# Two transformer blocks in one program: other order at the start, at each stage's end, in the RWKV scan and at the last store

## The reference, cut to what matters

```
for i in 0, 1:                                  # first block; mixer = gMLP, then RWKV-7
    h = h + 0.5 * rms_norm(swiglu(rms_norm(h, g[0]), w13, w2), g[1])      # ffn
    h = h + rms_norm(mixer(rms_norm(h, g[2])), g[3])
    h = h + 0.5 * rms_norm(swiglu(rms_norm(h, g[4]), w13', w2'), g[5])    # ffn
    gate = sigmoid(rms_norm(h, g[6]) @ w_gate)
    h = h + rms_norm(gate * (p[i] @ w_proj), g[7])                        # ple
# second block: the same form, mixer = dilated attention, then windowed GQA
rms_norm(x, g) = x * rsqrt(mean(x*x) + eps) * g
# RWKV-7: per head a 64 x 64 state, S_t = S_{t-1} diag(w) + (S_{t-1} a) b^T + v k^T, y_t = S_t r_t,
# then y minus its mean per head, times rsqrt of its variance, + bonus, times g, @ w_out
```

## Time and profile before

| | before |
|---|---|
| median of 3 runs, us | 2353.99 (2350.56 to 2355.45) |
| profiled execution: own time, us | 2350.35 |
| profiled execution: span, us | 2348.6 |
| mean granted TensorE clock | 0.984 |
| busy share of the span, PE / DVE / ACT / POOL | 96% / 63% / 49% / 8% |
| mean DMA rate, GB/s | 168 |

### The profile page before, as it was taken

The page is one execution under the profiler, slowest core; times in us unless marked ns, Lnnn a source line. Parts: engine busy times, 40 slices in busy tenths (PEclk is TensorE's granted clock), DMA queues, the critical chain, the costliest instruction groups (busy, mean ns, idle before and its releaser), DMA issues.

```text
span 2348.6 us, 33586 instructions
## 1 busy us (share of the span) xinstructions
PE 2251.9 (96%) x13285; PEld 1824.1 (78%) x13285; DVE 1471.0 (63%) x2077; ACT 1156.9 (49%) x1670; POOL 181.9 (8%) x289
## 2 busy tenths in 40 slices
PE   8999899999999899889999999999999999979998
PEld 6888788887888557768887888877887788748886
DVE  5656657656664866566657656656656765647655
ACT  5445445445544454244455445455445544545444
POOL 1001001001000110410011001001001000051001
PEclk9999999999999999899999999999999999989999
DMA  7556555554755540046456555524555655506553
GB/s 246 188 189 210 181 181 192 181 180 152 225 189 200 174 136 3 3 160 204 163 193 200 189 187 190 183 91 158 189 186 170 206 180 194 176 13 202 190 175 107
DMA packets 289755, 395.60 MB, mean 168 GB/s; under 512 B 11673, under 2 KB 193249, under 8 KB 289601
## 3 DMA queue, kind: packets, MB, share of 16 engines
q1 hardware_dynamic: 284752, 377.20, 48.4%
q0 software_dynamic: 4704, 16.20, 2.0%
q10 hardware_dynamic: 144, 0.07, 0.0%
HBM read 392.37 MB, written 1.05 MB: 168 GB/s over the span
## 4 chain that ended last, share of the span: by engine, by line
PE 78%; DVE 6%; ACT 2%; issue 2%; POOL 1%; DMA 0%; DVEq 0%; POOLq 0%; SPq 0%; ACTq 0%
PE bank L504 23%; PE bank L506 23%; PE bank L505 22%; PE bank L530 1%; DVE wl L800 1%; PE bank L518 1%; ACT wh L616 1%; DVE TMP L842 0%; ACT XH L628 0%; DVE H L862 0%; DVE qPS L1830 0%; PE bank L1404 0%; ACT JUNK L623 0%; PE bank L2471 0%; PE bank L2482 0%
## 5 line engine op out<-in xcount | busy, mean ns | idle before, releaser
L800 DVE TENSOR_TENSOR wl<-raw,wh 128x1024 fp32r<-128x1024 f32 x708 | 860.4, 1225 | 570.7 <-ACT wh L616 570.2
L616 ACT ACTIVATE wh<-raw 128x1024 fp32r<-128x1024 f32 x708 | 744.4, 1058 | 658.5 <-PE bank L506 630.1
L504 PE MATMUL bank<-wh,XH 128*128 128x512 f32 x2000 | 805.4, 403 | 18.5 <-ACT wh L616 6.0
L505 PE MATMUL bank<-wl,XH 128*128 128x512 f32 x2000 | 784.3, 392 | 0.0
L506 PE MATMUL bank<-wh,XL 128*128 128x512 f32 x2000 | 784.1, 392 | 0.0
L504 PEld LDWEIGHTS bank<-wh,XH 128*128 128x128 f32 x2000 | 378.5, 189 | 109.9 <-issue 19.4
L506 PEld LDWEIGHTS bank<-wh,XL 128*128 128x128 f32 x2000 | 378.4, 189 | 82.5
L505 PEld LDWEIGHTS bank<-wl,XH 128*128 128x128 f32 x2000 | 379.3, 190 | 73.3 <-issue 0.5
L504 PE MATMUL bank<-wh,AH 128*128 128x512 f32 x704 | 276.0, 392 | 0.0
L506 PE MATMUL bank<-wh,AL 128*128 128x512 f32 x704 | 274.1, 389 | 0.0
L505 PE MATMUL bank<-wl,AH 128*128 128x512 f32 x704 | 274.0, 389 | 0.0
(11 more groups left out here) (332 smaller groups left out, 1709.7 us busy)
## 6 DMA issues: line engine op xcount, KB each, us to landing
raw<-in_ffn_w_dram SPq DMA_DIRECT2D x184, 512.0 KB, 4.7
raw<-in_ffn_wi_dram SPq DMA_DIRECT2D x176, 512.0 KB, 4.7
raw<-in_ffn_w_dram SPq DMA_DIRECT2D x40, 1024.0 KB, 4.9
raw<-in_ffn_wo_dram SPq DMA_DIRECT2D x40, 1024.0 KB, 4.8
raw<-in_a_wqkv_dram SPq DMA_DIRECT2D x18, 1024.0 KB, 4.8
raw<-in_a_w_in_dram SPq DMA_DIRECT2D x16, 1024.0 KB, 6.1
raw<-in_b_w_in_dram SPq DMA_DIRECT2D x12, 1024.0 KB, 4.9
bc<-in_norm_g_dram POOLq DMA_DIRECT2D x16, 512.0 KB, 5.2
```

The lines of the kernel that those rows point to most:

```text
L504: pe.e.matmul(o, a, h, start=(k == 0), stop=False)
L505: pe.e.matmul(o, a, l, start=False, stop=False)
L616: act.e.activation(self.wh[j % N_W][:, 0:p.size], self.raw[p.chunk % N_RAW][:, p.at:p.at + p.size], ACT.Copy).then_inc(*self.rounded.up(j))
L800: dve.e.tensor_tensor(self.wl[j % N_W][:, 0:p.size], self.raw[p.chunk % N_RAW][:, p.at:p.at + p.size], self.wh[j % N_W][:, 0:p.size].bitca ...
```

## The change

- Start: SP loads tile 0, chunk 0 in four DMAs of 256 KB (part 0's two first, with a semaphore of their own), then tile 1, then the rest. TensorE turns only tile 0 ahead of the first step and tile 1 at steps 2 and 3. ACT and DVE put parts 0 and 1 ahead of tile 1.
- Stage ends: the sum of squares is a function of its own, `dve_mean`, ahead of `dve_weigh` of the second half. In PLE stages `dve_weigh` doesn't wait for the square. In the dilated stage the same for both tiles.
- Scan: both grams ahead of both `krv`; the banks are handed out from the pair after V's last one; the norm's segments are steps of their own and spread over levels 3 to 5 and `fin`; tile 1's bonus is made ahead of `seen 1`, into KK's tile 0; the leave of part 6 moves from `fin` into the tail; the tail's two halves are interleaved and TensorE's turns stand beside steps 15 and 19.
- End: four stores of 256 KB, each when its half has been added.

The diff, cut to its core:

```diff
     def pe_turn_own(self, pe, n, step):
 
-        if n and step == 6:
+        first = 6 if n else 2
+        if step == first:
             self.pe_turn_x(pe, n, 1, 0)
-        if n and step == 7:
+        if step == first + 1:
             self.pe_turn_x(pe, n, 1, 1)
...
+    def wait_raw(self, e, p):
+        if p.j:
+            e.wait_ge(self.d_raw[p.chunk % N_RAW], p.chunk)
+        else:
+            e.wait_ge(self.d_first, 1)
...
         for j in range(N_W):
+            if j < 2:
+                self.act_x_hi(act, 0, 0, j)
+            if j == 2:
+                for b in range(2):
+                    self.act_x_hi(act, 0, 1, b)
             self.round(act, j)
...
-        dve.wait_ge(self.squared, "out", n, b, t)
+        if STAGES[n][0] != "ple":
+            dve.wait_ge(self.squared, "out", n, b, t)
         dve.e.tensor_tensor(self.TMP[:, t, b, 512:1024], y, self.bct[g][:, b * 512:(b + 1) * 512],
                             ALU.mult).then_inc(*self.weighed.up(n, b, t))
...
-    def dve_resid(self, dve, n, t):
+    def dve_mean(self, dve, n, t):
...
+    def dve_resid(self, dve, n, t):
+
+        x = self.cols(T, "sm", n)[:, t:t + 1]
...
         for t in range(T):
+            self.dve_mean(dve, n, t)
             self.dve_weigh(dve, n, 1, t, self.pair((n, "out", 1))[t])
             self.dve_resid(dve, n, t)
...
         dve.e.memset(self.NEG[:, :], -0.5).then_inc(*self.neg.up())
         for b in range(2):
-            for t in range(T):
-                self.dve_x_scale(dve, 0, t, b)
-                self.dve_x_lo(dve, 0, t, b)
-        for j in range(N_W):
+            self.dve_x_scale(dve, 0, 0, b)
+        self.dve_x_lo(dve, 0, 0, 0)
+        self.leave(dve, 0)
+        self.dve_x_lo(dve, 0, 0, 1)
+        self.leave(dve, 1)
+        self.dve_x(dve, 0, 1)
+        for j in range(2, N_W):
             self.leave(dve, j)
...
+        if c == 0:
+            to = to.rearrange("p k (s n) -> p k s n", s=2)
+            for i, (k0, s) in enumerate(((0, 0), (0, 1), (2, 0), (2, 1))):
+                signal = self.d_first.up(s, by=16) if k0 == 0 else self.d_raw[0].up(*(("half", 0), (0,))[s], by=16)
+                sp.e.dma_start(to[:, k0:k0 + 2, s, :], src[:, k0:k0 + 2, s, :]).then_inc(*signal)
+            return
...
+        tokens(0)
...
+            if c == 0:
+                tokens(1)
...
-            sp.wait_ge(self.resid, n, t, 1)
-            sp.e.dma_start(self.out[0, t * P:(t + 1) * P, :], self.H[:, t, :]).then_inc(*self.d_out.up(t, by=16))
-        sp.wait_ge(self.d_out, T - 1)
+            for b in range(2):
+                sp.wait_ge(self.resid, n, t, b)
+                sp.e.dma_start(self.out[0, t * P:(t + 1) * P, b * 512:(b + 1) * 512],
+                               self.H[:, t, b * 512:(b + 1) * 512]).then_inc(*self.d_out.up(t, b, by=16))
+        sp.wait_ge(self.d_out, T - 1, 1)
...
-        for o in range(2):
-            steps += [("gram", 0, o), ("krv", 0, o)]
-        steps += [("complete", 0)]
+        steps += [("gram", 0, 0), ("gram", 0, 1), ("krv", 0, 0), ("krv", 0, 1), ("complete", 0)]
...
+        steps[-1:-1] = [("bonus", 1, 0), ("bonus", 1, 1)]
+        side = {1: [("state", 1), ("bonus", 0, 0), ("bonus", 0, 1)], 2: [("yo", 0)], 3: [("centre", 0, 0)],
+                4: [("square", 0, 0), ("centre", 0, 1)], 5: [("var", 0, 0), ("square", 0, 1), ("gain", 0, 0)]}
         for lv in range(1, 6):
             steps += [("level_a", 1, 0, lv), ("level_a", 1, 1, lv), ("level_b", 1, 0, lv), ("level_b", 1, 1, lv)]
             steps += side[lv]
-        steps += [("fin", 1, 0), ("fin", 1, 1), ("seen", 2), ("turn", 0, 0), ("turn", 0, 1), ("state", 2)]
+        steps += [("fin", 1, 0), ("var", 0, 1), ("gain", 0, 1), ("fin", 1, 1), ("scale", 0, 0), ("add", 0, 0),
+                  ("scale", 0, 1), ("add", 0, 1), ("seen", 2), ("turn", 0, 0), ("turn", 0, 1), ("state", 2)]
...
-    SCAN_TAIL = (("seen", 3), ("bonus", 1, 0), ("bonus", 1, 1), ("yo", 1), ("norm", 1, 0, 0, 6), ("norm", 1, 1, 0, 6),
-                 ("turn", 1, 0), ("turn", 1, 1))
+    SCAN_TAIL = (("seen", 3), ("part", 6), ("yo", 1), ("centre", 1, 0), ("square", 1, 0), ("centre", 1, 1), ("var", 1, 0),
+                 ("square", 1, 1), ("gain", 1, 0), ("var", 1, 1), ("gain", 1, 1), ("scale", 1, 0), ("add", 1, 0),
+                 ("scale", 1, 1), ("add", 1, 1), ("turn", 1, 0), ("turn", 1, 1))
+
+    SCAN_BESIDE = {2: ("seen", 3), 6: ("yo", 1), 15: ("turn", 1, 0), 19: ("turn", 1, 1)}
...
+        self.n_scan = self.place["pair", (n, "v", 1)] + 1
...
-            elif kind == "fin":
-                if tuple(a) == (1, 0):
-                    self.leave(dve, self.layers[n, "out"].parts[6].j)
+            elif kind == "part":
+                self.leave(dve, self.layers[n, "out"].parts[a[0]].j)
...
-        return self.AA if t == 0 else self.TB
-
-    def dve_scan_norm(self, dve, t, h, seg):
+        return self.AA[:, 0, :] if t == 0 else self.KK[:, 0, :]
...
-                    pool.wait_ge(self.product, "yo", 0)
+                    pool.wait_ge(self.product, "bt", 0, 1)
...
-            elif kind == "norm" and a[3] == 6:
-                t, h = a[:2]
+            elif kind == "var":
+                t, h = a
```

More of the change, by code:

```diff
@@ L399, in __init__ @@
         self.d_raw = [count(f"d_raw{i}") for i in range(N_RAW)]
+        self.d_first = count("d_first")
         self.d_bc = [count(f"d_bc{i}") for i in range(3)]
@@ L612, in round @@
         p = self.parts[j]
-        act.wait_ge(self.d_raw[p.chunk % N_RAW], p.chunk)
+        self.wait_raw(act, p)
         if j >= N_W:
@@ L798, in leave @@
         dve.wait_ge(self.rounded, j)
-        dve.wait_ge(self.d_raw[p.chunk % N_RAW], p.chunk)
+        self.wait_raw(dve, p)
         dve.e.tensor_tensor(self.wl[j % N_W][:, 0:p.size], self.raw[p.chunk % N_RAW][:, p.at:p.at + p.size],
@@ L1079, in sync, with tokens @@
             *self.d_g.up(by=16))
-        for t in range(T):
+        def tokens(t):
             sp.e.dma_start(self.H[:, t, :], self.A["x"][0, t * P:(t + 1) * P, :]).then_inc(*self.d_h[t].up(by=16))
+        tokens(0)
         rwkv = self.layers[5, "k"].parts[0].chunk
@@ L1583, in dve_dil_out @@
         parts = self.layers[n, "out"].parts
-        for b in range(2):
-            self.dve_weigh(dve, n, b, 0, self.pair((n, "out", b))[0])
+        self.dve_weigh(dve, n, 0, 0, self.pair((n, "out", 0))[0])
+        self.dve_mean(dve, n, 0)
+        self.dve_weigh(dve, n, 1, 0, self.pair((n, "out", 1))[0])
         self.dve_resid(dve, n, 0)
@@ L2366, in pe_rwkv_scan @@
     def pe_rwkv_scan(self, pe, n):
+        self.n_scan = self.place["pair", (n, "v", 1)] + 1
         for step in self.scan_steps():
             self.pe_scan(pe, *step)
-        beside = {2: 0, 6: 3, 14: 6, 15: 7}
         self.n_pairs = 0
         def during(step):
-            if step in beside:
-                self.pe_scan(pe, *self.SCAN_TAIL[beside[step]])
+            if step in self.SCAN_BESIDE:
+                self.pe_scan(pe, *self.SCAN_BESIDE[step])
             self.pe_turn_next(pe, n, "out", step)
@@ L2622, in act_rwkv_scan @@
                 self.act_decay(act, 1, a[0] - 3, [self.RK[0][:, :], self.RK[1][:, :], self.BT[:, :]])
-            elif kind == "norm" and a[2] == 0:
-                t, h = a[:2]
+            elif kind == "square":
+                t, h = a
                 c = slice(h * 512, (h + 1) * 512)
@@ L2689, in dve_rwkv_scan @@
                 self.dve_scan_complete(dve, *a)
-            elif kind == "norm":
-                t, h, first, end = a
-                for seg in range(first, end):
-                    self.dve_scan_norm(dve, t, h, seg)
+            elif kind in ("centre", "gain", "var", "scale", "add"):
+                self.dve_scan_norm(dve, kind, *a)
             elif kind == "turn":
@@ L2779, in dve_scan_norm @@
                 *self.made.up("centred_y", t, h))
-        elif seg == 2:
+        elif kind == "gain":
             dve.wait_ge(self.figured, "gl", t, h)
@@ L2783, in dve_scan_norm @@
             dve.e.tensor_tensor(x, x, self.GG[:, t, c], ALU.mult).then_inc(*self.made.up("yg", t, h))
-        elif seg == 3:
+        elif kind == "var":
             dve.wait_ge(self.moved, "sq", t, h)
             dve.e.tensor_reduce(var, self.per_head(sq), AX, ALU.add).then_inc(*self.made.up("var", t, h))
-        elif seg == 4:
+        elif kind == "scale":
             dve.wait_ge(self.rs, "gn", t, h)
```

20 lines of the change are left out of this document (8 added, 12 removed).

## The result

| | before | after |
|---|---|---|
| median of the runs | 2353.64 us (2350.56 to 2355.45) | 2322.97 us (2319.10 to 2329.22) |
| ratio | 1 | 0.987 (95%: 0.985 to 0.990) |
| profiled execution: own time, span | 2350.35, 2348.6 | 2319.10, 2317.3 |
| TensorE busy, mean granted clock | 96%, 0.984 | 97%, 0.988 |

Forecast 2325.5, range 2317 to 2338. The spans of the two profiled executions differ by 31.3 us, the sum said 28.0. The total held; several of its parts did not, and the two kinds of error nearly cancel: that the total came so close is in part luck. The first block is the profile page's line of busy times after.

A forecast was written before the change was run, and what follows sets the result against it. It took TensorE, 96% busy, as the bound, so only its waits and low-clock stretches could be won back. Terms summing to 28.0 us off 2350.4 gave 2322.4, plus 3 for the median of runs: 2325.5, range 2317 to 2338.

The forecast's parts named there:

- The start: First layer: first product 6.3 us earlier, at 9.9, then a gap until part 2 at 18.1; -1.6 us, bounds -3.2 and 0.
- The sum ahead of the product: Stage ends: 0.7 off each norm chain; -4.7 at three PLE ends, -0.7 after RWKV, -2.1 dilated, -1.2 elsewhere.
- The small ends: Four FFN to PLE ends and RWKV's entry: 0.25 us each from the earlier sum, -1.2 in all.
- rival (e): Stage ends: every chain waits for the power and the product was already hidden, so 9.4 stays away; 2335, chance 5%.
- Into the scan: Scan's entry: the 1.41 wait for V's copy and its follower go, grams precede KRV products; -3.1 us, bounds -1.7 and -3.6.
- The norm between the levels: Tile 1's scan: levels 4 and 5 give -7.2, the way to state 2 -2.1, the clock 1.0; -10.3, bounds -5, -11.
- Rival (a): Scan: GpSimd's moved bonus meets the grams, mask products at 0.9 or more; -19 instead of -28, 2334.5, chance 12%.
- The tail: After yo 1: interleaved halves make half 1 ready 5.0 earlier, turns partly open at steps 15 and 19; -3.0, bounds -2.2, -4.0.
- Step 15's products start at 1012.9: Tail: turn 0.66, high 0.60 and low 0.69 lie open, about 2.1 us, before the products at step 15.
- The end: Last PLE end and store: 0.7 off the chain, 0.6 from a 256 KB last store; -1.3 us, bounds -0.7 and -1.6.
- its own mark for being wrong: Scan, V's last product to RWKV's end: forecast wrong if it shrinks under 12 us; three fifths of the sum stands there.
- rival (d): Scan, 885 to 1002: the new order keeps TensorE at its low clock level, +60 us, 2386, chance 3%.

The follow-up runs named there:

- e5: The changed kernel run again with no further edit; 2322.47 us, ratio 0.9871 to the kernel before.
- e9: e7 with V's gate products at steps 11, 14, 17, 20, the read-out at step 4 and the last turn at step 17; 0.9844, 2316 us.
- e11: e2 with the wait for the squares kept ahead of the norm's product in the PLE stages; ratio 0.9963 to the kernel before.
- e2: The kernel before with only the squares summed ahead of the norm's product and, in PLE, no wait for the squares; ratio 0.9952, -11.3 us.
- e3: The kernel before with only the scan's part: banks, grams, bonus, spread norm and the tail's turns; ratio 0.9962, -8.9 us.
- e7: The changed kernel with seen 2 and the first turn's remainder ahead of the second half's scale and add, state 2 before the second turn; ratio 0.9850.
- e1: The kernel before with only the new start and the result stored in halves; ratio 0.9987, -3.1 us.
- e4: The kernel before with V's four gate products at steps 11, 14, 17, 20 instead of 7, 11, 15, 19; ratio 0.9983, -4.0 us.
- e10: e9 with a start that puts all six parts of the head ahead of tile 1's scaling, its turns at steps 9 and 10; 0.9822, 2310 us.
- e6: The changed kernel with the norm of tile 1's scan back in six pieces behind levels 3, 4 and 5; ratio 0.9889.
- e8: The changed kernel with second weights loaded ahead of tile 1, parts 2 and 3 ahead of its scaling, its turns at steps 6 and 7; ratio 0.9876.
- e12: e10 with V's four gate products back at steps 7, 11, 15, 19; ratio 0.9821, 2310.5 us.

## Why the prediction was right, and where not

**1. The start (-1.6).** The mechanism was right to a tenth: first product at 9.93 (9.9), part 2 at 18.24 (18.1), gap 2.00. The cut into four DMAs cost nothing that shows. The size depends on what the clock does behind the gap (part 2's product takes 0.77 and stands for the low level in e5, 0.47 in e9, behind 2.16 and 2.30): one and the same instruction (264.25 in before) stands at 264.3 to 265.3 in five traces with the old start and at 261.1 to 264.1 in six with the new one, in the mean -2.4 (264.7 and 262.3).

**2. The sum ahead of the product (-4.7, -0.7, -2.1, -1.2).** Right at the large ends, too small at the small ones. PLE waits 0.76 and 0.49 (0.8 and 0.45). Over the three PLE ends TensorE waits 4.0 less, not 4.7: the sum took 1.56 as the first wait of all three, and at the other two it was 1.36 and 1.35. After RWKV it gave 0.6; dilated 1.82 for 2.34 and no product of 0.63 behind it, 2.0 in all. The small ends were mis-sized: the sum had 1.2 for five of them and nothing for the rest, and laid side by side the two traces differ by 0.2 to 0.55 at each of eleven, 4.6 in all. Most of it lies where, in before, tile 1's second turn or the first product that needs it waited about 0.2. (A PLE end together with the 0.4 that stands ahead of it shifts by 1.9, 1.7 and 1.7.) e11 shows that in PLE the gain hangs on the wait removed; rival (e) is false (e2).

**3. Into the scan (-3.1).** Measured 3.2 in the two traces of the changed kernel and in e3 (from V's last product to the KRV wait); the one KRV wait left is 1.35. In the trace of after this stretch shows 6.4, because V's layer ran at the full clock behind its short wait.

**4. The norm between the levels (-10.3).** Mis-sized: 7.1 in after and 9.1 in e5. Levels 4 and 5 gave 7.5 (7.2 forecast). What failed is the step from level 5 to state 2: 8.8 instead of 7.4 (957.7 to 966.5 in after), since the second power took 2.09 and its small operation 0.70, and the wait for it was 2.29; and the 1.0 us of clock that was to be spared was paid in after and e3 (1.97 for seen 3), not in e5. The rows of GpSimd after:

```profile
959.78 1.65 POOL L1003 TENSOR_TENSOR rSM<-rSM,NEG 128x8 f32<-128x8 f32 x1
961.52 0.70 POOL L1001 TENSOR_SCALAR rSM<-rSM 128x8 f32<-128x8 f32 x1
962.30 2.09 POOL L1003 TENSOR_TENSOR rSM<-rSM,NEG 128x8 f32<-128x8 f32 x1
```

The bonus beside the grams cost nothing: tile 0's levels and tile 1's grams are within 0.4, and DVE's mask products beside it took 0.67 to 0.73, not 0.9. Rival (a) is false. The KRV products behind them wait 1.21 as before.

**5. The tail (-3.0 and 0.7 of RWKV's end).** The step that failed: "Step 15's products start at 1012.9" stood for 2.1 of open latency. It was 3.11, with products 0.43 apart behind it. I had counted turn, high and low part, but not that in DVE's order the low part of half 0 comes behind scale and add of half 1, and with them behind the second power. e7 takes that away; e9 shows that the gain comes only once the clock stays up. Tail and RWKV's end gave 1.3 in after and 2.0 in e5, of the 3.7 forecast.

**6. The end (-1.3).** 1.6 (from the last stage's turn, 2314.95 and 2285.25, to the span's end). From the last gate product to the last sum it is 3.06 before (2341.06 to 2344.12) and 2.39 after (2310.99 to 2313.38), 0.67 for the 0.7 forecast, and 0.55 comes from the last sum's start to the span's end (4.48 and 3.93) for the 0.6; each store lands 2.1 after its issue. Another 0.4 is that of a small end, and the rest of the table's last row lies at the turns ahead of it.

The prediction named its own mark for being wrong: from V's last product to RWKV's end, a scan that shrinks by less than 12. In after it shrank by 11.6 (884.64 to 1031.29 against 875.57 to 1010.67), so by that mark the forecast is wrong there, just; in e5 it shrank by 13.9 (881.45 to 1014.22). The 16.4 that the sum had for it came in neither. What filled the hole was not in the sum. In after it was V's layer with the scan's entry, 5.1 us more than in e5, which is chance, since e5 is the same kernel. In both it was the small ends (3.4 over the 1.2) and GQA's output layer (1.6). Without these two the sum of e5 would have been 5 us short: its nearness to 28.0 is luck.

**GQA** stays open; it is the whole of the 1.6. It runs in two ways: with a wait of 2.7 to 2.9 before the output layer and low products behind it (before, e1, e3, e4, e7, e9, e10), or with 1.0 to 1.3 and none (e2, e11, after, e5, e6, e8, e12). All without the reordered sum run the long way, but three with it as well. The edit may shift the odds; no run settles it.

## What to carry to other kernels

Where TensorE is nearly always busy, price each wait together with what the clock does behind it: e7's tail took 1.6 us of waiting away and gave 0.4, since the low level lasted longer (twelve products against eight); e9's took 2.9 more away and gave 5.5 (37.65 and 32.11 from seen 3 to RWKV's end). On an engine that works in order, look at what is queued behind each wait you keep, and for whom; removing a gap by reordering (e8) only moves it until every item that TensorE needs stands ahead of the turning point (e10). And before a difference is put down to an edit, look whether a stage that the edit doesn't touch differs too: two executions of one kernel (after and e5) differed by 5.1 us over V's layer and the scan's entry.

## What the runs showed of the hardware

- TensorE's clock behind a gap follows no single length. It fell to the low level behind 2.00 (start, after), 2.29 (965.89), 2.34 (dilated, before), behind 1.98 (RWKV's end, e3) and behind 1.95 and 1.50 with four transposes between (e7). It held behind 1.97 (RWKV's end, before), 2.12 (state 2, e5) and 2.30 (start, e9: the product behind it took 0.47). And in e9 and e10 it ran at 0.50 for about 16 us in the scan, where the longest earlier wait of the scan was 1.35 and the waits were those of e7. The nearest thing to rival (d) thus did appear, at 7 us.
- GpSimd's power of 128x8 took 1.64 to 1.66 us as the first and 2.08 to 2.09 as the second of two in a row; the small operation ahead of it took 0.19 or 0.20 in before and at tile 0 in e6, 0.56 and 0.70 in after. DVE's gain product beside the first power (988.74 in after) did not lengthen it, so the cause isn't shown.
- A load of 128 KB on GpSimd's queue was followed by the product that waits for it 5.4 to 7.4 us after its issue, beside the weights' stream, in the eleven traces.
